# Merge region of a two-block forward pass: memory loaded in the region before, four banks for the means, halves taken as they come, variance and gatings placed one part earlier

## What is computed

```python
    y = rwkv7_recurrence(r, decay, k, v, -kk, kk * a)
    mean = jnp.mean(y, axis=-1, keepdims=True)
    var = jnp.mean(jnp.square(y - mean), axis=-1, keepdims=True)
    y = ((y - mean) * lax.rsqrt(var + LNX_EPS)).reshape(bsz, s, A_WIDTH) * lnx_g + lnx_b
    bonus = jnp.sum(r * k * r_k, axis=-1, keepdims=True) * v
    return (y + bonus.reshape(bsz, s, A_WIDTH)) * g
...
        merged = (jax.nn.sigmoid(proj[..., cb2:cg1]) * y_a
                  + jax.nn.sigmoid(proj[..., cg1:]) * y_b)
        x = x + merged @ w_mix_out[l]
        x = x + cross_attention(rms_norm(x, norm_x_g[l]), rms_norm(mem, norm_mem_g[l]),
                                w_cq[l], w_ckv[l], w_co[l])
```

## Time and profile before

| | us |
|---|---|
| median of 3 runs | 2733.44 (2733.4 to 2737.92) |
| profiled execution | 2730.76 |
| its span | 2729.0 |
| PE busy in the span | 2521.6 (92%) |
| DVE, ACT, POOL busy | 1439.8, 1023.3, 413.1 |
| mean granted clock of TensorE | 0.961 |

### The profile page before, as it was taken

The page is one execution under the profiler, slowest core; times in us unless marked ns, Lnnn a source line. Parts: engine busy times, 40 slices in busy tenths (PEclk is TensorE's granted clock), DMA queues, the critical chain, the costliest instruction groups (busy, mean ns, idle before and its releaser), DMA issues. The chain is left out here.

```text
span 2729.0 us, 31020 instructions
## 1 busy us (share of the span) xinstructions
PE 2521.6 (92%) x12166; PEld 1995.1 (73%) x12166; DVE 1439.8 (53%) x2076; ACT 1023.3 (37%) x1535; POOL 413.1 (15%) x367
## 2 busy tenths in 40 slices
PE   8989888998999999969989989999989988999997
PEld 5667776776788888747778866877767756687775
DVE  5476454544466632554423646677342364667743
ACT  4753335334333222325223544222233465422223
POOL 4545310010100000000034340000030143000002
PEclk9999998999999999989987998999999988899999
DMA  6325123320223333122210021222332201122231
GB/s 209 111 70 157 46 82 104 112 96 29 77 101 102 99 89 97 62 70 79 91 43 13 1 85 56 91 93 91 107 101 91 95 9 54 55 92 93 91 107 58
DMA packets 98032, 225.67 MB, mean 83 GB/s; under 512 B 28249, under 2 KB 44905, under 8 KB 96699
## 3 DMA queue, kind: packets, MB, share of 16 engines
q1 hardware_dynamic: 84776, 206.65, 23.4%
q10 hardware_dynamic: 13112, 17.04, 1.9%
HBM read 215.46 MB, written 13.43 MB: 84 GB/s over the span
## 5 line engine op out<-in xcount | busy, mean ns | idle before, releaser
L236 DVE TENSOR_TENSOR w_low<-w_raw,w_high 128x1024 fp32r<-128x1024 f32 (+2 forms) x337 | 405.8, 1206 | 850.6 <-ACT w_high L226 850.4
L298 PE MATMUL bank<-x_high,w_high 128*128 128x512 f32 x1840 | 744.2, 404 | 37.8 <-DVE x_low L492 20.4
L299 PE MATMUL bank<-x_low,w_high 128*128 128x512 f32 x1840 | 735.0, 399 | 0.0
L300 PE MATMUL bank<-x_high,w_low 128*128 128x512 f32 x1840 | 733.8, 399 | 0.0
L226 ACT ACTIVATE w_high<-w_raw 128x1024 fp32r<-128x1024 f32 (+2 forms) x380 | 386.1, 1019 | 581.7 <-PE bank L300 448.3
L298 PEld LDWEIGHTS bank<-x_high,w_high 128*128 128x128 f32 x1840 | 350.0, 190 | 146.5 <-issue 58.2
L299 PEld LDWEIGHTS bank<-x_low,w_high 128*128 128x128 f32 x1840 | 350.0, 190 | 87.9 <-issue 5.1
L300 PEld LDWEIGHTS bank<-x_high,w_low 128*128 128x128 f32 x1840 | 349.5, 190 | 83.4
L298 PE MATMUL bank<-f_high,w_high 128*128 128x512 f32 x528 | 209.8, 397 | 0.9 <-DVE w_low L236 0.9
L299 PE MATMUL bank<-f_low,w_high 128*128 128x512 f32 x528 | 209.2, 396 | 0.0
L300 PE MATMUL bank<-f_high,w_low 128*128 128x512 f32 x528 | 208.5, 395 | 0.0
(11 more groups left out here) (626 smaller groups left out, 3608.7 us busy)
## 6 DMA issues: line engine op xcount, KB each, us to landing
w_raw<-in_ffn_in_dram SPq DMA_DIRECT2D x132, 512.0 KB, 3.2
w_raw<-in_ffn_out_dram SPq DMA_DIRECT2D x48, 512.0 KB, 3.5
w_raw<-in_gdn_in_dram SPq DMA_DIRECT2D x24, 512.0 KB, 3.2
w_raw<-in_mix_in_dram SPq DMA_DIRECT2D x22, 512.0 KB, 4.4
w_raw<-in_ffn_out_dram SPq DMA_DIRECT2D x24, 384.0 KB, 3.1
w_raw<-in_swa_qk_dram SPq DMA_DIRECT2D x12, 512.0 KB, 3.2
bias_rows<-bias_row ACTq DMA_DIRECT2D x4, 1280.0 KB, 14.1
w_raw<-in_mix_gate_a_dram SPq DMA_DIRECT2D x8, 512.0 KB, 3.2
```

Of the source, the lines that this page charges most:

```text
L236: (on or self.nc.vector).tensor_tensor(self.low[c % SPLIT][:, 0:w], self.raw[c % RAW][:, 0:w], self.high[c % SPLIT][:, 0:w].bitcast(F32), ...
L298: nc.tensor.matmul(out, wh, high[:, k, :], start=first + at == 0, stop=False)
L299: nc.tensor.matmul(out, wh, low[:, k, :], start=False, stop=False)
L300: last = nc.tensor.matmul(out, wl, high[:, k, :], start=False, stop=first + at == depth - 1)
```

## The change

It does the following.

- The raw memory lies in three tiles at other places and is loaded by SP in `first_recurrence_region`, in three transfers, with a semaphore that lives across the regions.
- The four means have four banks: 6, 7 and the two that the second group of keys will use. They wait for nothing; `bonus` waits for the centrings instead.
- ACT does all eight `mem_high` first and the eight `mem_sq` behind them. DVE does two `mem_low` behind each centring. TensorE waits for 2 of them ahead of part 0 and for 4, 6 and 8 at the ends of parts 0, 1 and 2.
- The second square of `Y` waits for the memory to be used up, since its tile is now where part of the memory lies.
- The fourth variance goes from part 9 to part 8, `cols` from 8 to 9. The fourth logarithm, the exponentials and the first load of `gate_b` go from part 10 to part 9 on ACT, the columns and first keys from 9 to 10. Scalings go from parts 11 and 12 to 10 and 11, the products from 12 to 15 to 11 to 14, each `y_high` and all but the last `y_split` one part earlier.

```diff
+    mem = {k + i: tile[:, i, :] for tile, k, n in keep["mem"] for i in range(n)}
+    mean_banks = [6, 7] + [(W.unit["ck", 1, t]) % BANKS for t in range(2)]
...
-            sp.dma_start(mem[:], A["mem"]).then_inc(R["mem_in"], 16)
...
             def mean(j):
+                nc.tensor.matmul(PS[mean_banks[j]][:], C["pair_mean"][:], Y[:, j, :], start=True, stop=True).then_inc(
+                    R["mean"], 1)
+
+            def bonus(j):
+                pe.wait_ge(R["centred"], min(NA, 2 * j + 2))
                 if j >= 2:
-                    pe.wait_ge(R["centred"], j - 1)
...
+                    pe.wait_ge(R["valued"], j - 1)
...
                 if part == 8:
                     pe.wait_ge(R["y_ln"], 2)
+                    var(3, 6)
+                if part == 9:
+                    pe.wait_ge(R["y_ln"], 3)
                     pe.wait_ge(R["mem_rstd"], 2)
...
-                if part == 9:
-                    pe.wait_ge(R["y_ln"], 3)
-                    var(3, 7)
                 if part == 10:
-                    pe.wait_ge(R["cols_ok"], 1)
+                    pe.wait_ge(R["y_ln"], 4)
                     pe.wait_ge(R["squashed"], 1)
                     gate(0, 6)
                 if part == 11:
-                    pe.wait_ge(R["y_ln"], 4)
+                    pe.wait_ge(R["cols_ok"], 1)
                     gate(1, 7)
...
-            pe.wait_ge(R["mem_low"], ND)
+            def beside_keys(part):
+                beside(part)
+                if part < 3:
+                    pe.wait_ge(R["mem_low"], 2 * part + 4)
+
+            pe.wait_ge(R["mem_low"], 2)
...
-            act.wait_ge(R["mem_in"], 16)
+            act.wait_ge(keep["mem_in"], 16 * len(keep["mem"]))
...
+            for kk in range(ND):
                 if kk >= 2:
                     act.wait_ge(R["mem_acc"], kk - 1)
...
             def square(j):
                 act.wait_ge(R["centred"], j + 1)
+                if j == 1:
+                    act.wait_ge(R["mem_low"], ND)
+                    act.wait_ge(R["mem_sq"], ND)
...
-                if part in (13, 14, 15):
-                    j = part - 13
+                if part >= 12:
+                    j = part - 12
                     act.wait_ge(R["y"], j + 1)
...
             for j in range(NA):
                 dve.wait_ge(R["mean"], j + 1)
...
+                mem_rest(2 * j)
+                mem_rest(2 * j + 1)
...
-                if part in (11, 12):
-                    scaled(2 * part - 22)
-                    scaled(2 * part - 21)
-                if part >= 12:
-                    gated(part - 12, 6 + part % 2)
-                if part >= 14:
-                    y_split(part - 14)
-            y_split(2)
+                if 11 <= part < 15:
+                    gated(part - 11, 6 + (part + 1) % 2)
+                if part in (10, 11):
+                    scaled(2 * part - 20)
+                    scaled(2 * part - 19)
+                if part >= 13:
+                    y_split(part - 13)
             y_split(3)
...
+            for tile, k, n in keep["mem"]:
+                sp.dma_start(tile[:], A["mem"][:, k:k + n, :]).then_inc(keep["mem_in"], 16)
...
+                 "mem": [(E.at("mem_raw", kb, P, n, NMEM), k, n) for kb, k, n in ((32, 0, 4), (96, 4, 2), (102, 6, 2))]}
```

More of the change, by code:

```diff
@@ L1254, in merge_region @@
     g_lora = E.at("g_lora", 24, P, A_WIDTH)
-    mem, rows = E.at("mem_raw", 92, P, ND, NMEM), E.at("k_rows", 28, P, 2, ND, P)
+    rows = E.at("k_rows", 28, P, 2, ND, P)
     mem_high, mem_low = (E.at(n, kb, P, ND, NMEM, dtype=F32R) for n, kb in (("mem_high", 76), ("mem_low", 84)))
@@ L1267, in merge_region @@
     c0, parts = W.first("ck"), 16
-    with region(nc, "mem_in", "x_in", "g_in", "a_in", "b_in", "squashed", "mean", "centred", "bonus", "valued", "y_sq",
+    mem = {k + i: tile[:, i, :] for tile, k, n in keep["mem"] for i in range(n)}
+    mean_banks = [6, 7] + [(W.unit["ck", 1, t]) % BANKS for t in range(2)]
+    with region(nc, "x_in", "g_in", "a_in", "b_in", "squashed", "mean", "centred", "bonus", "valued", "y_sq",
                 "var", "y_ln", "y_rstd", "normed", "gated", "y", "y_high", "y_low", "yb_high", "yb_low", "mem_high",
@@ L1284, in mean @@
             def mean(j):
-                if j >= 2:
-                    pe.wait_ge(R["centred"], j - 1)
-                nc.tensor.matmul(PS[6 + j % 2][:], C["pair_mean"][:], Y[:, j, :], start=True, stop=True).then_inc(
+                nc.tensor.matmul(PS[mean_banks[j]][:], C["pair_mean"][:], Y[:, j, :], start=True, stop=True).then_inc(
                     R["mean"], 1)
             def bonus(j):
-                if j < 2:
-                    pe.wait_ge(R["centred"], 3 + j)
-                else:
+                pe.wait_ge(R["centred"], min(NA, 2 * j + 2))
+                if j >= 2:
                     pe.wait_ge(R["valued"], j - 1)
@@ L1364, in _ @@
                 mean(j)
-            pe.wait_ge(R["mem_low"], ND)
+            def beside_keys(part):
[3 more added lines that the diff above has]
+            pe.wait_ge(R["mem_low"], 2)
             for g in range(2):
-                W.sums_rows(pe, PS, "ck", g, tokens, mem_high, mem_low, beside)
+                W.sums_rows(pe, PS, "ck", g, tokens, mem_high, mem_low, beside_keys)
             for g in range(2):
@@ L1442, in _ @@
                     log(2, 7)
-                if part == 9:
+                if part == 10:
                     act.wait_ge(R["cols"], 1)
-                    nc.scalar.activation(cols[:], PS[6][:, 0:2], ACT.Copy).then_inc(R["cols_ok"], 1)
+                    nc.scalar.activation(cols[:], PS[7][:, 0:2], ACT.Copy).then_inc(R["cols_ok"], 1)
                     act.wait_ge(R["cols_ok"], 1)
                     evacuate("ck", 0, lambda g, t: rows[:, t, 4 * g:4 * g + 4, :])
-                if part == 10:
-                    log(3, 7)
+                if part == 9:
+                    log(3, 6)
                     for j in range(NA):
@@ L3960, in build @@
         merge_region(nc, C, W, PS, A, E, x, (gate_a, gate_b), {
[L3961 removed]
+            "M": M, "YB": YB, "Y": Y, "q": q, "k": k, "v": v, "mem": first["mem"], "mem_in": first["mem_in"]})
         o = E.at("o", 0, P, ND, S)
```

23 lines of the change are left out of this document (10 added, 13 removed).

## The result

The changed kernel took 2708.48 us (median of 4 runs, 2704.49 to 2709.29) beside 2735.68 for the kernel before (4 runs): a ratio of 0.9898, 95% interval 0.9881 to 0.9915. That is 27.2 us less, where 27.6 were forecast, and inside the range. In a second comparison, on another occasion, the ratio was 0.9907 (0.9892 to 0.9923). Both intervals leave out 1.

What follows compares the result with a forecast made beforehand. TensorE's 20.5 us of waits for mem_low and VectorE's products, plus low clock behind them, were taken as the bound. Gains 7.0 + 2.7 + 17.9 = 27.6 us gave 2705.8 us against the 2733.4 median; range 2700 to 2713.5.

Steps and rivals of the forecast that it cites:

- Waiting at the start: Start of the merge region: TensorE's wait for the last mem_low, between the means and first key matmul, disappears; 7.0 us.
- Clock at the start: From first key matmul to second bonus: TensorE goes on without a pause at full clock; 2.7 us gained.
- about 5.4 us after the first mean: Sign at the start: the first key matmul comes this long after the first mean, without a wait for mem_low.
- Four banks 0, squares moved 0, `cols` and `var(3)` exchanged 0: Means, ScalarE's memory squares and the middle parts: these three moves each gain or cost 0.
- Three loads in the region before, 0: Start of the recurrence: three load issues of about 0.33 us each on SyncE, costed at 0.
- ScalarE late with the split after the squares, 0.5 us: End of part 0: squares end near 403, the next weights' split is 0.5 us late; covered by three parts, cost 0.
- The gatings, 17.9: From part 12's end to first branch_b matmul: 17.9 us gained, 11.3 of it waiting and 6.6 clock and restarts.
- `gate_b`: Second half of gate_b arrives at 477.6, VectorE wants it at about 478.2; lateness would cost TensorE 0.
- VectorE was the bound of the gatings: Rival: lateness in VectorE's full chain lands on TensorE, 0.7 us more per wait plus low clock, 3 to 5 us; chance 0.17.
- Kinder clock: Rival: waits of 1.4 us never drop the clock, low stretch in the means vanishes; 2702.5 us; chance 0.10.
- The halves came in time: Rival denied here: TensorE waits for mem_low 2, 4 or 6, 2 us plus 2.7 of clock, 2710.5 us; chance 0.06.
- The clock didn't stay low: Rival denied here: clock at 1.2 GHz from part 0 to the end of part 15, 2764 us; chance 0.02.

Runs made afterwards that it cites:

- the start without the gatings: Changed kernel with variance, exponentials, scalings, products and splits of Y put back where they were before; 84.85 us from first mean to first branch_b matmul.
- squares between: Changed kernel with each square of the memory right behind its high half on ScalarE; 69.35 us from first mean to first branch_b matmul.

## Why the prediction was right

- **Waiting at the start, 7.0 us:** 12.37 − 4.80 = 7.6, by the distance of the first key matmul from the first mean. I read the end of the means as start plus duration (5.37); the next matmul starts 4.80 behind, since the end in such a row overlaps the next instruction. For the same reason the sign "about 5.4 us after the first mean" was 4.80.
- **Clock at the start, 2.7:** 9.9 − 7.6 = 2.3. Of the two terms one was 0.6 too small and the other 0.4 too large, for the same reason: the first key part took 3.21 us (399.79 to 403.00) and not 2.82, since its first row begins while the last mean still runs. The errors made up for each other, so that the sum of the start, 9.7 for 9.9, is better than its terms. "I give it the full clock" held: 1.00 from 399.8 on.
- **Four banks 0, squares moved 0, `cols` and `var(3)` exchanged 0:** the first two were shown by undoing them; of the third no run tells more than that no wait stands there. `cols_ok` was there at 443.56, 0.8 us ahead of the gating at 444.36 that asks for it, as in the forecast (0.7).
- **Three loads in the region before, 0:** no wait of an engine in that region is for them. The load alone gives 3.2 of the start, and the forecast did not say so: it priced the start as a whole and not by moves. The halves alone were not run.
- **ScalarE late with the split after the squares, 0.5 us:** the squares ended at 404.3 and not near 403; the split began at 404.18, more than 1 us behind the end of part 0 (403.0), and still cost nothing.
- **The gatings, 17.9:** 17.8. The waits were 1.27, 0.17 and 0.28 by their brackets, for 1.4, 0.4 and 0.4. The forecast reckoned from the end of a part, 0.24 us behind the start of its last matmul, and so counted they are 1.42 (449.45 − 448.03), 0.33 (453.55 − 453.22) and 0.43 (462.83 − 462.40): each link was right. Of its 6.6 us for the clock and restarts no experiment isolates the part of the clock. In the start without the gatings the same four waits cost 0.8 us less, since low clock held for less long behind the longest; that it came out as priced is in part luck.
- **`gate_b`:** VectorE multiplies with it at 469.26 without a wait.
- **Rivals.** VectorE was the bound of the gatings only as far as the 1.4 us of the forecast. With the product 2.9 us later it cost 4.8 us, so the mechanism of that rival is real, and the price of 3 to 5 us for 0.7 at each wait was not tested. "Kinder clock" was half right: waits of 1.3 us didn't bring it down, but the low stretch in the means stayed; that one is a draw. The halves came in time. The clock didn't stay low.
- **The time, 2705.8:** measured 2708.5 and 2705.9. The forecast started from 2733.4 for before; beside the changed kernel before took 2735.7 and 2731.8. In the first comparison that is 2.3 of the 2.7 us by which the forecast is off. The ±4 us for the clock outside were needed: the profiled execution gave back 4.0 there.

The Trainium skill states in TensorE: Matmul & The Clock Gate, Part 1, that the window of the activity monitor is free-running and that the point of transition varies with it. The traces agree, without showing the cause: the same 2.04 us of idle time ahead of the same four means was followed by a low stretch in ten executions (means of about 5.4 us) and by none in three (3.67 us).

## What to carry to other kernels

When a value is loaded earlier, read what else the consumer's engine has in its list ahead of it: here the load alone gave a third, and the rest came once TensorE asked for two halves and not for eight (4.6 of 9.9 us), and VectorE made them between the centrings. Where one engine waits for a chain of another, put the product that frees it ahead of whatever nobody waits for yet, and look for idle time of that engine just ahead of the chain. Look at the waits of TensorE's weight loads too; one of them was missing in the view of its matmuls. Judge such an edit on its stretch, since the rest of the program varies by more than most single moves bring. Two executions of one kernel agreed to 0.02 us there, but the level of the clock in the means alone moved other stretches by 1.7 us, so read the clock with it.

## What the runs showed of the hardware

- A wait of TensorE cost more than its bracket in the timeline: about 0.25 us, of which 0.16 is the counting from the row's end, and where it was 2 us or more often a piece at the lower clock. Waits of 4.2 and 4.5 us were followed by 0.59 and 0.54; those of 1.3 us, in six executions, by 1.00.
- Two low halves of the memory took 0.88 us while GpSimd was idle and 1.71 beside its sums, in the same place of the program (changed kernel, squares between).
- The part of the program that no experiment touched took 2630.9 to 2641.2 us, a spread of 10 us or 0.4%.
